# Paged forgetting attention: heads two at a time, decays added on VectorE, first cache pages loaded during the prompt part

## The reference

```python
def fox_attend_prompt(q, k, v, logf):
    Fk = jnp.cumsum(logf, axis=1).transpose(0, 2, 1)
    ...
        s = jnp.einsum('bqhd,bkhd->bhqk', qi, k, preferred_element_type=F32) * scale
        s = s + Fq[..., :, None] - Fk[..., None, :]
        s = jnp.where(kpos[None, :] <= qpos[:, None], s, -jnp.inf)
        p = jax.nn.softmax(s, axis=-1)
        return jnp.einsum('bhqk,bkhd->bqhd', p.astype(v.dtype), v)
...
def fox_attend_sample(q, k, v, logf, pool_k, pool_v, pool_lf, page_table):
    k_past = pool_k[page_table].reshape(B, -1, H, Dh)
    ...
    k_all = jnp.concatenate([k_past.astype(k.dtype), k], axis=1)
```

## Time and profile before

| | |
|---|---|
| runs | 4428.03 us median of 3 (4427.86 to 4439.33) |
| profiled execution, span | 4393.3 us; the page gives no other time of that execution |
| runs' median less the span | 34.7 us |
| prep, prompt, sample (us from the start) | 966.9 to 1026.3, to 1274.3, to 1512.4 |
| the three together | 59.4 + 248.0 + 238.1 = 545.5 us |
| PE over the span | 88% busy, granted clock mostly 0.7 to 1.0 |

### The profile page before, as it was taken

One profiled execution on the slowest core, in us unless ns is written; L12 is line 12 of the kernel. 1 busy time (PEld: TensorE's weight loads), 2 busy tenths in 40 slices (PEclk: granted clock), 3 DMA queues, 4 the chain that ended last, 5 costly groups with the idle time before them and its releaser, 6 DMA issues. The chain is left out here.

```text
span 4393.3 us, 64529 instructions
## 1 busy us (share of the span) xinstructions
PE 3858.2 (88%) x23932; PEld 3576.1 (81%) x23932; DVE 2228.7 (51%) x4008; ACT 940.1 (21%) x1746; POOL 1229.2 (28%) x930
## 2 busy tenths in 40 slices
PE   8997688857989889999999799867886889999997
PEld 8997477746753489999999699766785879999996
DVE  3254688433220226655556566327764166565654
ACT  2000333125332211111111222113442021111112
POOL 4221233222000123323332133214443243333331
PEclk9999788767689899999999899887886989999998
DMA  5244211022026211111110122222214121111111
GB/s 176 82 154 165 64 54 26 5 85 72 1 86 205 77 38 53 50 36 53 33 53 24 32 94 92 84 72 64 73 37 106 38 58 34 54 37 53 33 43 49
DMA packets 365848, 290.63 MB, mean 66 GB/s; under 512 B 100831, under 2 KB 326175, under 8 KB 365333
## 3 DMA queue, kind: packets, MB, share of 16 engines
q1 hardware_dynamic: 317624, 231.15, 18.1%
q10 hardware_dynamic: 48060, 57.33, 3.8%
HBM read 216.39 MB, written 73.99 MB: 66 GB/s over the span
## 5 line engine op out<-in xcount | busy, mean ns | idle before, releaser
L982 PE MATMUL fup_acc<-ffn_high,fup_wh 128*128 128x364 f32 (+1 forms) x2112 | 699.8, 331 | 46.8 <-POOL fup_wl L906 42.5
L983 PE MATMUL fup_acc<-ffn_low,fup_wh 128*128 128x364 f32 (+1 forms) x2112 | 698.5, 331 | 0.0
L984 PE MATMUL fup_acc<-ffn_high,fup_wl 128*128 128x364 f32 (+1 forms) x2112 | 696.1, 330 | 0.0
L982 PEld LDWEIGHTS fup_acc<-ffn_high,fup_wh 128*128 128x128 f32 x2112 | 400.4, 190 | 48.9 <-POOL fup_wl L906 41.3
L1163 DVE TENSOR_TENSOR trunk_xT<-fup_dn,trunk_xT 128x364 f32<-128x364 f32 x528 | 282.7, 535 | 255.1 <-PE fup_dn L1014 255.1
L983 PEld LDWEIGHTS fup_acc<-ffn_low,fup_wh 128*128 128x128 f32 x2112 | 400.8, 190 | 0.0
L984 PEld LDWEIGHTS fup_acc<-ffn_high,fup_wl 128*128 128x128 f32 x2112 | 400.5, 190 | 0.0
L1012 PE MATMUL fup_dn<-fup_gh,fup_dh 128*128 128x364 f32 (+1 forms) x1056 | 346.9, 328 | 0.0
L1013 PE MATMUL fup_dn<-fup_gl,fup_dh 128*128 128x364 f32 (+1 forms) x1056 | 345.9, 328 | 0.0
L1014 PE MATMUL fup_dn<-fup_gh,fup_dl 128*128 128x364 f32 (+1 forms) x1056 | 345.4, 327 | 0.0
L335 PE MATMUL p_acc<-p_wh,even_in_high 128*128 128x296 f32 (+1 forms) x936 | 281.4, 301 | 10.5 <-DVE even_in_low L374 7.9
(11 more groups left out here) (718 smaller groups left out, 8459.2 us busy)
## 6 DMA issues: line engine op xcount, KB each, us to landing
fup_ws<-in_ffn_w_up SPq DMA_DIRECT2D x88, 512.0 KB, 3.9
fup_ds<-in_ffn_w_down SPq DMA_DIRECT2D x22, 1024.0 KB, 5.9
fs_kp<-in_cache_fox_k SPq DMA_DIRECT2D x64, 256.0 KB, 2.9
fs_vp<-in_cache_fox_v SPq DMA_DIRECT2D x64, 256.0 KB
ev<-p_o ACTq DMA_DIRECT2D x104, 148.0 KB, 1.8
p_ws<-in_ev_w_in SPq DMA_DIRECT2D x12, 1184.0 KB, 6.9
qkv<-gqkv_conv ACTq DMA_DIRECT2D x24, 544.0 KB, 2.7
gqkv_ws<-in_od_w_in SPq DMA_DIRECT2D x24, 512.0 KB, 4.1
```

The lines of the kernel that those rows point to most:

```text
L982: pe.matmul(ps, wh[:, b, k], xh[:, k, c0:c0 + w_], start=(k == 0), stop=False)
L983: pe.matmul(ps, wh[:, b, k], xl[:, k, c0:c0 + w_], start=False, stop=False)
L984: mm = pe.matmul(ps, wl[:, b, k], xh[:, k, c0:c0 + w_], start=False, stop=(k == KD - 1))
```

## The change

Four functions and their calls in `trunk` change. Decays no longer ride in the matmuls: q and k hold two heads in 128 rows (`qk`), the cumulated decays go through DRAM (`fd`, `fds`) into tables of 128 rows (`F`), and one DVE instruction (`tensor_tensor_reduce`) adds them to the scores and takes the minimum of the row. In the prompt a unit n covers both heads of a pair (32 units): scores of head 0 and head 1 use rows 0 to 63 and 64 to 127 of the array, values columns 0 to 63 and 64 to 127. In the sample part the 8 heads stand in 4 column tiles of 32, two heads in each. The cache blocks (8 pages each) go through a ring of 5 slots, of which SP fills 3 in the prompt part. The residual is read back in `project_back`.

```diff
+            if kept is not None:
+                half = KD // 2 * NTOK
+                for q in range(2):
+                    act.dma_start(xT.rearrange("p k t -> p (k t)")[:, q * half:(q + 1) * half],
+                                  kept[:, q * half:(q + 1) * half]).then_inc(x_in[q], 16)
...
+            if kept is not None:
+                for q in range(2):
+                    dve.wait_ge(x_in[q], 16)
...
+                    sp.wait_ge(F_done, 1)
+                    sp.dma_start(fd.rearrange("h (n k) -> (h n) k", k=P), FT[:]).then_inc(F_out, 16)
...
+                for m in range(H):
+                    mm = pe.transpose(ps[i % 2][:, m, :r], qn[:r, i % 2, 2 * m:2 * m + 2].rearrange("p h d -> p (h d)"),
+                                      C["ident"][:r, :r])
...
+            def decays_in(i):
+                if i >= 2:
+                    sp.wait_ge(decayed, 2 * NT * (i - 1))
+                for q in range(2):
+                    sp.dma_start(F[:, i % 2, q, :], fd[2 * i + q].partition_broadcast(P)).then_inc(F_in[i % 2], 16)
             sp.dma_start(table[:], page_table.rearrange("b n -> (b n)").unsqueeze(0)).then_inc(table_in, 16)
+            decays_in(0)
+            decays_in(1)
...
+            for j in range(3):
+                for g in range(NPG):
+                    sp.dma_start(kv[j][:, g, :], pools[j % 2][bass.ds(page_of(j // 2 * NPG + g), 1)]
+                                 .rearrange("o p c -> p (o c)")).then_inc(kv_in[j][g // HALF], 16)
...
                 sp.dma_start(lp[:, n % NPG, n // NPG * H:(n // NPG + 1) * H],
-                             pool_lf[bass.ds(page, 1)].rearrange("o p h -> p (o h)")).then_inc(l_in, 16)
+                             pool_lf[bass.ds(page_of(n), 1)].rearrange("o p h -> p (o h)")).then_inc(l_in, 16)
+            decays_in(2)
+            decays_in(3)
...
+                pool.tensor_tensor(sr[:, n % 2], sog[:, qt, i * P:(i + 1) * P].rearrange("p (q d) -> p q d", q=2),
+                                   bc(ri[:, n, :], 2, DH), ALU.mult).then_inc(gated, 1)
...
+            def score(n):
+                i, qt = divmod(n, NT)
+                L = length(n)
+                if n:
+                    pe.wait_ge(decayed, 2 * n)
...
+                    for q in range(2):
+                        rows = slice(q * DH, (q + 1) * DH)
+                        pe.matmul(S[:, 2 * q + c0 // 512, :w], qk[rows, i, qt * P:(qt + 1) * P],
+                                  qk[rows, turns + i, c0:c0 + w], start=True, stop=c0 + w < L)
+                for q in range(2):
+                    pe.matmul(S[:, 2 * q + (L - 1) // 512, (L - P) % 512:(L - P) % 512 + P], unit[:], mask[:],
+                              start=False, stop=True).then_inc(scored, 1)
...
+            def turn(n):
+                qt = n % NT
+                for c in range(chunks(n)):
+                    for q in range(2):
+                        if c == 0:
+                            pe.wait_ge(expd, 2 * n + q + 1)
+                        if chunks_to(n) + c:
+                            pe.wait_ge((copied_a, copied_b)[q], chunks_to(n) + c)
+                        for kt in range(4 * c, min(4 * c + 4, qt + 1)):
+                            mm = pe.transpose(psT[:, q, kt % 4 * P:(kt % 4 + 1) * P],
+                                              sc[:, n % 2, q, kt * P:(kt + 1) * P], C["ident"][:])
+                        mm.then_inc(turned, 1)
...
+                pe.wait_ge(copied_a, chunks_to(n + 1))
+                pe.wait_ge(copied_b, chunks_to(n + 1))
...
+                    for q in range(2):
+                        rows = slice(q * DH, (q + 1) * DH)
+                        mm = pe.matmul(psO[rows, qt % 4 * P:(qt % 4 + 1) * P],
+                                       v[:, kt, (2 * i + q) * DH:(2 * i + q + 1) * DH], pT[:, q, kt, :],
+                                       start=(kt == 0), stop=(kt == qt))
...
+            def turn_gate(n):
+                qt = n % NT
+                pe.wait_ge(gated, n + 1)
+                if qt % 4 == 0 and n:
+                    pe.wait_ge(mixed, n // 4)
+                pe.transpose(psG[:, qt % 4 * P:(qt % 4 + 1) * P], sr[:, n % 2].rearrange("p q d -> p (q d)"),
+                             C["ident"][:]).then_inc(gate_turned, 1)
...
+                turn(n)
+                if n + 2 < U:
+                    score(n + 2)
+                value(n)
+                turn_gate(n)
...
+            def decay(n, q):
+                i, L = n // NT, length(n)
+                if n % NT == 0 and q == 0:
+                    dve.wait_ge(F_in[i % 2], 32 * (i // 2 + 1))
+                if n >= 2 and q == 0:
+                    dve.wait_ge(turned, 2 * chunks_to(n - 1))
+                dve.wait_ge(scored, 2 * n + q + 1)
+                dve.tensor_tensor_reduce(sc[:, n % 2, q, :L],
+                                         S[:, 2 * q:2 * q + 2, :].rearrange("p c x -> p (c x)")[:, :L],
+                                         F[:, i % 2, q, :L], -1.0, 3.0e38, ALU.add, ALU.min,
+                                         accum_out=mx[:, n, q:q + 1]).then_inc(decayed, 1)
+            def invert(n):
...
+            def load(j):
+                if j >= SLOTS:
+                    i, part = divmod(j - SLOTS, 2)
+                    if part:
+                        sp.wait_ge(valued, i + 1)
+                    else:
+                        sp.wait_ge(k_turned, 8 * (i + 1))
...
+                    n = j // 2 * NPG + g
+                    page = sp.value_load(table[0:1, n:n + 1], min_val=0, max_val=N_POOL - 1)
+                    sp.dma_start(kv[j % SLOTS][:, g, :], pools[j % 2][bass.ds(page, 1)].rearrange("o p c -> p (o c)"))\
+                        .then_inc(kv_in[j % SLOTS][g // HALF], 16)
...
+            step(pool.memset(F[:], 0.0))
+            pool.wait_ge(F_out, 16)
+            for h in range(H):
+                r = 32 * (h // 2) + TS * (h % 2)
+                pool.dma_start(F[r:r + TS], fds.rearrange("(b h) k -> h b k", h=H)[h].partition_broadcast(TS))\
+                    .then_inc(F_in, 16)
+            pool.wait_ge(F_in, 16 * H)
...
+            def score(i, c):
+                if c == 0 and i:
+                    pe.wait_ge(maxed, i)
+                pe.wait_ge(k_even, 4 * i + 2 * c + 2)
+                pe.wait_ge(k_odd, 4 * i + 2 * c + 2)
...
+                    mm = pe.matmul(PS[32 * m:32 * m + 32, c, :], qx[:, i, m, :], kT[:, 4 * c + m, :], start=True,
+                                   stop=True)
...
+                    pe.transpose(PX[:, g * P:(g + 1) * P], sc[:, g * P:(g + 1) * P], ident[:])
+                pe.transpose(PN, sc[:, PAST:], ident[:]).then_inc(p_turned, 1)
...
+                for g in range(NPG + 1):
+                    for m in range(4):
+                        src = values_of(i)[:, g, m * P:(m + 1) * P] if g < NPG else vn[:, i % 2, m * P:(m + 1) * P]
+                        mm = pe.matmul(O[32 * m:32 * m + MR], pT[:, g, m, :], src, start=(g == 0), stop=(g == NPG))
+                mm.then_inc(valued, 1)
...
+            act.dma_start(fds, Fn[:]).then_inc(F_out, 16)
...
+            dve.wait_ge(F_set, 1)
+            def decay(i):
+                dve.wait_ge(scored, i + 1)
+                if i:
+                    dve.wait_ge(p_turned, i)
+                dve.tensor_tensor_reduce(sc[:], S, F[:, i, :], -1.0, 3.0e38, ALU.add, ALU.min,
+                                         accum_out=mx[:, i:i + 1]).then_inc(maxed, 1)
...
-            project_back(nc, "back0", (foxT, rwT), mh, ml, I["ev_w_out"][0], xT)
+            project_back(nc, "back0", (foxT, rwT), mh, ml, I["ev_w_out"][0], xT, None, x_kept)
```

More of the change, by code:

```diff
@@ L705, in project_back @@
         m_high, m_low = ph.sem("m_high"), ph.sem("m_low")
+        x_in = [ph.sem(f"x_in{q}") for q in range(2)]
         block = ph.block()
@@ L1412, in _, with chunks, chunks_to, length @@
+        def chunks(n):
+            return n % NT // 4 + 1
+        def chunks_to(n):
+            return sum(chunks(m) for m in range(n))
+        def length(n):
+            return (n % NT + 1) * P
         @block.sync
         def _(sp):
+            def decays_in(i):
+                if i >= 2:
+                    sp.wait_ge(decayed, 2 * NT * (i - 1))
+                for q in range(2):
+                    sp.dma_start(F[:, i % 2, q, :], fd[2 * i + q].partition_broadcast(P)).then_inc(F_in[i % 2], 16)
@@ L1507, in _, with exp, copy_probs @@
-            act.sem_inc(copied, 1)
-            for i in range(turns):
-                body(i)
+            def exp(n, q):
+                L = length(n)
+                act.wait_ge(decayed, 2 * n + q + 1)
+                act.activation(sc[:, n % 2, q, :L], sc[:, n % 2, q, :L], ACT.Exp, bias=mx[:, n, q:q + 1], scale=-1.0,
+                               accum_out=rs[:, n, q:q + 1]).then_inc(expd, 1)
+            def copy_probs(n, c):
+                w = min(4, n % NT + 1 - 4 * c)
+                if c == 0 and n:
+                    act.wait_ge(valued, n)
```

(46 more changed lines are left out.)

592 lines of the change are left out of this document (258 added, 334 removed).

## The result

The changed kernel takes 4285.01 us (median, 4276.29 to 4289.94) against 4427.94 for the one before: a ratio of 0.9689 (95% interval 0.9645 to 0.9732). The forecast was 4260, its range 4210 to 4365.

What follows compares the result with a forecast made beforehand. PE bounds the prompt and sample parts, nothing bounds prep. Stages of 545.5 us become 56.4 + 185.5 + 134 + 2 = 377.9; 167.6 off the 4393.3 span gives 4225.7, plus 34.7: 4260 us, range 4210 to 4365.

Steps and rivals of the forecast that it cites:

- the wait for the tables behind 64 small loads: Prompt, pair 2: DVE waits for decay tables queued on SP, leaving PE idle some 20 to 30 us.
- SP's pages: Sample part: SP's page loads bound the stage, 16 pages or about 16.6 us a sequence.
- a sign of being wrong: Sample part: the prediction would be wrong if a sequence takes over 18 us.
- the first and third rivals: First: columns in turn, 4356 us, chance 0.14. Third: columns in turn at a low clock, 4611 at 0.50, chance 0.05.
- the second: Rival: clock 0.50 throughout with columns side by side, 4398 us, chance 0.07.
- what a pair costs at a given clock: Prompt, PE: 29.4 us a pair divided by the clock, plus 2.8; 39.6 at clock 0.80.
- the waits for the copies of transposes: Prompt, PE: units above four blocks wait for a copy, 0.7 us in four units, 2.8 a pair.
- I take 11: Sample part: the eight decay broadcasts issued by POOL, 2.1 MB, priced at 11 us.
- in turn at 2.9 each 23: Sample part: alternative price of the eight broadcasts if they go one after another, 23 us.
- the first values: Sample part: the first values' matmuls end at about 39 us into the stage, range 33 to 48.
- Projection: Projection back: residual now read at its start, beside weights; 0 to +5 us, taken as +2.
- The 34.7 us "around" the span: Whole kernel: median of runs less the profiled span, 34.7 us, added to 4225.7 to give the forecast time.

Runs made afterwards that it cites:

- e1: Changed kernel with pair 2's decay tables issued ahead of the 64 small loads, pair 3's still behind them: 4260.5 us.
- e3: Changed kernel with SP's page loads of the sample part held back until the decay table has landed: 4292.9 us (one run).
- e11: e10 with the residual's two transfers issued only when the projection's first weights have landed: 4218.8 us.
- e10: Changed kernel with pair 2's tables before the small loads, the sample part's table in three groups, pages looked up once per sequence: 4227.0 us.

## Why the prediction was right, and by how much it was not

**The mechanism.** Both new bounds were the forecast ones: the wait for the tables behind 64 small loads (24.95 us, forecast 20 to 30), then SP's pages (17.95 us a sequence for 16.6, just under the 18 that was named as a sign of being wrong). The columns ran side by side, which sets the first and third rivals aside; the clock was 0.88 and 0.78, which sets the second aside.

**Prep**: from its first load to the prompt's, 57.1 before and 55.2 now, -1.9 (forecast -3).

**Prompt**: 195.7 for 185.5. The tables came at 106.4 in place of 103.5. Pairs 0 and 1 were done at 81.6 for 84, and that is luck: the clock was 0.93 there, where 0.80 was taken, and at 0.93 the sum gives 73 (the prediction's 74 at full clock should be 69). Pairs 2 and 3 took 89.2 for 82 although the clock of that half was 0.95 where 0.80 was taken: the mis-sized term is what a pair costs at a given clock. In e1, where nothing else holds it up, four pairs take 176.8 at a clock of 0.91, some 42 each, where the sum gives 29.4 / 0.91 + 2.8 = 35. Passes of values cost 0.059 and not 0.053, 0.8 us for a pair's 144; the waits for the copies of transposes are 4 and not 2.8; and a wait that I had not priced, the gate's transpose for DVE's multiplication, adds 11.4 us over the part. That is 5 of the 7 us; the rest is not accounted for.

**Sample**: 162.1 for 134. The failed term is "I take 11" for the eight broadcasts: 32.0. It was priced at the 380 GB/s of the earlier trace rows, but two thirds of the bytes of that stretch were the residual's one large transfer, in pieces of 34 KB, and not the two blocks that the prediction names. The bound "in turn at 2.9 each 23" is what they take alone (23.2, e3), and the pages beside them add 9; with both, the first values end at 56.7 us, outside the 33 to 48 of the range. Nine blocks took 80.3 in place of 74.7 us (+5.6), the tail 24.5 for 20.5.

**Projection**: +7.1 for +2, outside the bound of +5. I had named the weights beside the residual, but what I priced was DVE's wait for the residual; what came was PE's wait for the first weights, and it goes when the residual is issued later (e11).

**The base.** The 34.7 us "around" the span do not exist: in the runs whose span is known the time is 1.7 to 2.3 us above it. The profiled execution of before was a short one; other executions of the same kernel had spans from 4363.5 (clock 0.913) to 4439.2 (0.894), most of them above 4398. From the profiled span the stages give -1.9 - 52.3 - 76.0 + 7.1 = -123, and the two spans differ by 105.5: 6.2 us are lost before the change's stages and 11.3 after PE's start in the projection, nearly all of it in code that did not change. Against the median the gain is 143. The forecast of -167.6 was too large by either, and the sum's errors, all on one side, are 45 us. That the time came out only 25 above the forecast is luck of the base and not a merit of the sum: the other 20 are the difference between 143 by the medians and 123 by the stages.

## What to carry to other kernels

When a change frees the busiest engine, read the queue that feeds what comes next: here the order of transfers on one queue was worth 19 us, and moving work "under" a part cost more than it saved because it stood ahead of something needed; with the needed transfer put first, the same work was a gain. A table that is brought in whole, though its first eighth is needed first, should be cut where it is consumed. A small look-up before each transfer can pace a stage that looks bound by bandwidth: leave it out once and see.

## What the runs showed of the hardware

In float32, two column tiles of 64 columns side by side cost 0.059 us a pass against 0.101 in turn (1.7 times), four column tiles of 16 used columns 0.027 against 0.098 (3.6 times). The time of the same 2.1 MB went with the rows of a transfer: 50.8 us in transfers of 4 rows, 32 apart, and 32.0 in transfers of 8 neighbouring rows with pages beside them, 23.2 of 8 alone, and 5.2 in four of 128 rows. A block of pages that was issued beside the broadcasts was slow too: 23.3 us to landing where 3.0 is usual. A look-up in the page table costs SP some 0.5 us a page: eight page loads take 8.0 to 8.4 us with it and 4.0 to 5.1 without (e10, once the rings carry pages alone).
